# A hybrid decoder step on one core: score tiles spread over the ticks, low parts of q and k stored by their own stage, convolution rows joined, PV emptied by ScalarE alone

## What is computed

```python
q = rmsnorm(q, q_norm); k = rmsnorm(k, k_norm)            # per head, 16 heads of 64
logits = q @ k.T * ATTN_SCALE + bias                      # three dilated windows, merged
o = softmax(logits) @ v
out = sum(xpad[:, i:i + t] * conv_w[i] for i in range(4)) + conv_b
xbc = silu(out); z = silu(z)
```

## Time and profile before

| | us |
|---|---|
| median of 3 runs (2239.98 to 2244.58) | 2243.39 |
| the profiled execution | 2248.43 |
| span of its trace | 2245.8 |
| TensorE busy | 2100.7 (94%) |
| VectorE busy | 1047.1 (47%) |
| ScalarE busy | 588.3 (26%) |
| POOL busy | 840.3 (37%) |
| mean granted TensorE clock, share of 2.4 GHz | 0.971 |

### The profile page before, as it was taken

The page is one execution under the profiler, slowest core; times in us unless marked ns, Lnnn a source line. Parts: engine busy times, 40 slices in busy tenths (PEclk is TensorE's granted clock), DMA queues, the critical chain, the costliest instruction groups (busy, mean ns, idle before and its releaser), DMA issues. The chain is left out here.

```text
span 2245.8 us, 30116 instructions
## 1 busy us (share of the span) xinstructions
PE 2100.7 (94%) x12136; PEld 1845.0 (82%) x12136; DVE 1047.1 (47%) x1452; ACT 588.3 (26%) x1055; POOL 840.3 (37%) x494
## 2 busy tenths in 40 slices
PE   8999997898888899699998899999999999999999
PEld 7999996677777778345454678999999999999999
DVE  5888605778787665235443655252222122221222
ACT  4333223544455554232322201121101011010110
POOL 3564304646656655122211212333333333333332
PEclk9999998999999999789999899999999999999999
DMA  4333315333233341854744443311111111111112
GB/s 157 122 140 144 124 50 122 93 102 90 86 104 100 104 114 33 261 173 156 261 162 172 161 169 113 123 34 57 38 47 47 47 47 37 47 47 47 47 37 96
DMA packets 102756, 230.70 MB, mean 103 GB/s; under 512 B 17195, under 2 KB 50475, under 8 KB 101116
## 3 DMA queue, kind: packets, MB, share of 16 engines
q1 hardware_dynamic: 90252, 188.38, 26.8%
q10 hardware_dynamic: 12400, 40.90, 5.0%
HBM read 187.52 MB, written 50.29 MB: 106 GB/s over the span
## 5 line engine op out<-in xcount | busy, mean ns | idle before, releaser
L818 POOL TENSOR_SCALAR att_p<-att_p,att_rden 128x128 f32<-128x128 f32 (+7 forms) x128 | 229.3, 1793 | 227.1 <-DVE att_rden L916 226.9
L1847 POOL CAST wo_hi<-wo_raw 128x1024 fp32r<-128x1024 f32 x64 | 66.8, 1043 | 492.3 <-issue 239.4
L2171 ACT ACTIVATE r_sq<-stage 128x1056 f32<-128x1056 f32 x32 | 34.8, 1088 | 623.7 <-DVE stage L2360 623.7
L1849 POOL TENSOR_TENSOR wo_lo<-wo_raw,wo_hi 128x1024 fp32r<-128x1024 f32 x64 | 187.7, 2933 | 5.1
L1051 ACT ACTIVATE att_p<-att_p,att_min 128x128 f32<-128x128 f32 (+7 forms) x128 | 99.4, 776 | 152.0 <-DVE att_min L933 151.8
L921 DVE TENSOR_TENSOR att_pTlo<-att_t_ps,att_pThi 128x512 fp32r<-128x512 f32 x192 | 106.2, 553 | 54.9 <-ACT att_pThi L1059 52.8
L843 PE MATMUL dense_ps<-u_hi,w_hi 128*128 128x352 f32 x480 | 120.4, 353 | 11.7 <-DVE silu_half L961 4.7
L1059 ACT ACTIVATE att_pThi<-att_t_ps 128x512 fp32r<-128x512 f32 x192 | 92.0, 479 | 94.9 <-PE att_t_ps L872 94.0
L843 PE MATMUL dense_ps<-u_hi,w_lo 128*128 128x352 f32 x480 | 113.1, 345 | 0.0
L843 PE MATMUL dense_ps<-u_lo,w_hi 128*128 128x352 f32 x480 | 113.0, 346 | 0.0
L611 DVE RECIPROCAL proj_rinv<-proj_rinv 128x1056 f32<-128x1056 f32 x16 | 108.0, 6753 | 9.8 <-ACT proj_rinv L504 9.8
(11 more groups left out here) (307 smaller groups left out, 5355.6 us busy)
## 6 DMA issues: line engine op xcount, KB each, us to landing
sa_k<-in_cache_k SPq DMA_DIRECT2D x32, 640.0 KB, 9.2
sa_v<-in_cache_v SPq DMA_DIRECT2D x40, 512.0 KB, 7.0
w_raw<-in_w_feat SPq DMA_DIRECT2D x36, 512.0 KB, 6.1
wo_raw<-in_w_up SPq DMA_DIRECT2D x32, 512.0 KB, 3.5
wo_raw<-in_w_down SPq DMA_DIRECT2D x32, 512.0 KB, 3.5
out_qk<-proj_out ACTq DMA_DIRECT2D x16, 528.0 KB, 10.1
tmp_bias_rows<-tmp_table ACTq DMA_DIRECT2D x8, 1024.0 KB
att_q<-out_qk SPq DMA_DIRECT2D x32, 256.0 KB, 4.7
```

Of the source, the lines that this page charges most:

```text
L818: pool.tensor_scalar(slot(h, qt), slot(h, qt), rden[:, qt, :], None, ALU.mult).then_inc(normed, 1)
L1849: pool.tensor_tensor(w_lo[:, j], raw_w, w_hi[:, j].bitcast(F32), ALU.subtract).then_inc(f_split[j], 1)
```

## The change

- The score tiles move: qt 0 and 1 in tick 4, 2 and 3 in tick 5, qt 7 in tick 7, 4 in tick 9, 5 in tick 10, 6 in tick 12. qt 7 has two slots of its own (even and odd heads). A tile's number in the semaphores is now `rank`.
- `project` also makes a high copy of each normed q and k tile (ScalarE), subtracts it (POOL, `split_qk`) and stores the low part to a new DRAM tensor `qk_low` (ScalarE's queue). `split_k` and `split_q` are gone from VectorE. `weave` loads the raw tile in partitions 0 to 63 and the low tile in 64 to 127, for k and q. ScalarE makes four copies per head where it made two. The first product takes q's high part twice against k's high and low part, the second q's low part against k's high part over 64 rows (the product low x low is gone). The number of matmuls and their columns stay.
- The convolution's sample columns stand behind the prompt columns in one buffer of 1083 columns, so that a tap is one VectorE instruction over 1080 columns; the small copies of past and tail rows go to POOL (`pad`, `keep_tail`). The four taps of a tile go to the least loaded of the five ticks after its eviction.
- The product with zeros is gone: the last piece's product of the high part closes the accumulation. ScalarE copies both halves of PV (`split_out`), TensorE waits for those copies (`o_split`), and VectorE adds them later from SBUF.
- The order in a tick: VectorE `keep_low`, `bias_min`, `invert`, `evict`, `add_out`, `split_v`, taps, gates; ScalarE `split_out`, `keep_high`, `exponent`, casts, tanh, stores.
- The last z tile's tanh, gate and store run in three column groups.
- project and weave are two parts for the semaphores; POOL clears project's in tick 0 of `weave`.

```diff
@@ project
+                def split_qk(t):
+                    pool.wait_ge(highs_made, t + 1)
+                    if t >= 1:
+                        pool.wait_ge(lows_stored, 16 * t)
+                    pool.tensor_tensor(lows[:], outs[:, t % 2, 0:SEQ], high[:].bitcast(F32),
+                                       ALU.subtract).then_inc(lows_made, 1)
...
                 for n in range(3, NQ + 1):
                     ring.split_part(kit, pool, n, 0, 1)
+                    if n >= 4:
+                        split_qk(n - 4)
                     split_sq(n - 2)
...
                 def store(t):
                     act.wait_ge(normed, t + 1)
                     act.dma_start(dram["qk"][t * P:(t + 1) * P, :], outs[:, t % 2, :]).then_inc(qk_stored[t % 2], 16)
+                    if t >= 1:
+                        act.wait_ge(lows_made, t)
+                    act.activation(high[:], outs[:, t % 2, 0:SEQ], ACT.Copy).then_inc(highs_made, 1)
+
+                def store_low(t):
+                    act.wait_ge(lows_made, t + 1)
+                    act.dma_start(dram["qk_low"][t * P:(t + 1) * P, :], lows[:]).then_inc(lows_stored, 16)
...
                     evict(t)
+                    if t >= 3:
+                        store_low(t - 3)
                     store(t - 2)
...
                     if t >= 2:
                         dve.wait_ge(qk_stored[t % 2], 16 * (t // 2))
+                        dve.wait_ge(lows_made, t - 1)
@@ weave
+RANK = (0, 1, 2, 3, 5, 6, 7, 4)
+SCORE_TICK = (4, 4, 5, 5, 9, 10, 12, 7)
+SLOTS = (0, 128, 384, 768, 1280, 1920, 2688, 3584, 4608)
...
-            n = TICKS * (h - 1) + 5 + qt if qt < HALF else TICKS * (h - 1) + 5 + qt
-            score[n] = (h, qt)
+        for qt in sorted(range(NT), key=lambda q: RANK[q]):
+            score.setdefault(TICKS * (h - 1) + SCORE_TICK[qt], []).append((h, qt))
...
+    for d in range(ND):
+        evict_at.setdefault(made_at[d], []).append(d)
+        last = made_at[d]
+        if d < NX:
+            free = sorted(range(last + 1, last + 6), key=lambda n: (busy[n], n))[0:WIDTH]
...
-                    for rows in (slice(0, HD), slice(HD, P)):
-                        sp.dma_start(q_raw[rows, :], dram["qk"][f * P + r:f * P + r + HD, 0:SEQ]).then_inc(qk_loaded, 16)
...
+                        sp.wait_ge(qk_cast, 4 * h)
+                    for buf, first in ((k_raw, D + f * P + r), (q_raw, f * P + r)):
+                        sp.dma_start(buf[0:HD, :], dram["qk"][first:first + HD, 0:SEQ]).then_inc(qk_loaded, 16)
+                        sp.dma_start(buf[HD:P, :], dram["qk_low"][first:first + HD, :]).then_inc(qk_loaded, 16)
...
+                    for d in evict_at.get(n - 1, ()):
+                        if d < NX:
+                            keep_tail(d)
+                    for d in tanh_at.get(n, ()):
+                        if d + 1 < NX:
+                            pad(d + 1)
...
+                    if n == 0:
+                        kit.clear(pool)
...
-                def scores(s, h, qt):
+                def scores(h, qt):
+                    free = NT * h + max(qt - 1, 0) if qt < HALF else rank(h, qt)
                     if qt == 0:
-                        pe.wait_ge(qk_split, h + 1)
+                        pe.wait_ge(qk_cast, 4 * (h + 1))
+                    if free:
+                        pe.wait_ge(biased, free)
...
-                        pe.matmul(s_ps[:, base + c:base + c + cw], q, k_hi[:, c:c + cw], start=True, stop=False)
-                        mm = pe.matmul(s_ps[:, base + c:base + c + cw], q, k_lo[:, c:c + cw], start=False, stop=True)
+                        pe.matmul(out, q_high[:, qt * P:w], k_two[:, c:c + cw], start=True, stop=False)
+                        mm = pe.matmul(out, q_low[:, qt * P:w], k_two[0:HD, c:c + cw], start=False, stop=True)
...
-                            pe.wait_ge(o_kept, 2 * h + g)
+                            pe.wait_ge(o_split, 2 * h + g)
...
-                    if b == HALF * (g + 1) - 1:
-                        mm = pe.matmul(pv_ps[:], nought[:], x_hi[:, 0, 0:512], start=False, stop=True)
+                    if last:
+                        mm = pe.matmul(pv_ps[:, off:512], v_two[:, h % 2, b, :], p_hi[:, m % 3, off:512],
+                                       start=False, stop=True)
...
-                    dve.tensor_tensor(oT[h % 2 * HD:(h % 2 + 1) * HD, g * 512:(g + 1) * 512], pv_ps[0:HD, :], o_part[:],
-                                      ALU.add).then_inc(o_kept, 1)
+                    dve.tensor_tensor(oT[h % 2 * HD:(h % 2 + 1) * HD, g * 512:(g + 1) * 512], o_parts[:, 0, :],
+                                      o_parts[:, 1, :], ALU.add).then_inc(o_kept, 1)
...
-                        dve.scalar_tensor_tensor(out=acc_p, in0=pre[:, t:t + SEQ], scalar=w, in1=acc_p,
-                                                 op0=ALU.mult, op1=ALU.add)
-                        dve.scalar_tensor_tensor(out=acc_s, in0=pre_s[:, :, t:t + T_DEC], scalar=w, in1=acc_s,
-                                                 op0=ALU.mult, op1=ALU.add).then_inc(conv, 1)
+                        dve.scalar_tensor_tensor(out=half[:, 0:CONV], in0=pre[:, t:t + CONV], scalar=w,
+                                                 in1=half[:, 0:CONV], op0=ALU.mult, op1=ALU.add).then_inc(conv, 1)
...
-                def split_k(h):
-                    dve.wait_ge(qk_cast, 2 * h + 1)
-                    dve.tensor_tensor(k_lo[:], k_raw[:], k_hi[:].bitcast(F32), ALU.subtract)
-
-                def split_q(h):
-                    dve.wait_ge(qk_cast, 2 * h + 2)
-                    dve.tensor_tensor(q_two[HD:P, :], q_raw[HD:P, :], q_two[HD:P, :].bitcast(F32),
-                                      ALU.subtract).then_inc(qk_split, 1)
...
-                    act.activation(o_part[:], pv_ps[HD:P, :], ACT.Copy).then_inc(o_split, 1)
+                    act.activation(o_parts[:, 0, :], pv_ps[0:HD, :], ACT.Copy)
+                    act.activation(o_parts[:, 1, :], pv_ps[HD:P, :], ACT.Copy).then_inc(o_split, 1)
...
-                    act.activation(k_hi[:], k_raw[:], ACT.Copy).then_inc(qk_cast, 1)
-
-                def cast_q(h):
-                    act.activation(q_two[:], q_raw[:], ACT.Copy).then_inc(qk_cast, 1)
+                    act.activation(k_two[:], k_raw[:], ACT.Copy).then_inc(qk_cast, 1)
+
+                def cast_q(h, rows):
+                    act.activation(q_high[rows, :], q_raw[0:HD, :], ACT.Copy).then_inc(qk_cast, 1)
+
+                def cast_q_low(h):
+                    act.activation(q_low[:], q_raw[HD:P, :], ACT.Copy).then_inc(qk_cast, 1)
...
+                        act.dma_start(rows[:, 0:SEQ], half[:, 0:SEQ]).then_inc(feat_stored, 16)
+                        act.dma_start(rows[:, SEQ:NTOK].rearrange("p (b t) -> p b t", b=NB_DEC),
+                                      sample(half)[:, :, 0:T_DEC]).then_inc(feat_stored, 16)
```

More of the change, by code:

```diff
@@ L265, in project @@
         out = outs[:, 0, :]
+        high, lows = sb("qk_high", [P, SEQ], F32R), sb("qk_low", [P, SEQ])
         x_eps = sb("x_eps", [P, NTOK])
@@ L676, in weave, with rank, width @@
     UNITS = 3 * KD
-    order = {s: 8 * h + qt for s, (h, qt) in score.items()}
+    END = LAST + 12
+    def rank(h, qt):
+        return NT * h + RANK[qt]
+    def width(n):
+        _, g, b = piece[n]
+        return P * (HALF - max(b - HALF * g, 0))
     def pe_cost(n):
@@ L713, in weave, with stores @@
                 made_at[d] = n
-    at = {}
-    for d, n in made_at.items():
-        at.setdefault(n, []).append(d)
-    starts = {}
-    for d in range(1, ND):
-        starts[made_at[d - 1]] = d
-    END = LAST + 9
+    starts = {made_at[d - 1]: d for d in range(1, ND)}
+    ends = {n + 3: piece[n][0:2] for n in piece if piece[n][2] == HALF * (piece[n][1] + 1) - 1}
+    busy = dict.fromkeys(range(FIRST, END + 1), 0.0)
+    for n in busy:
+        if n in piece:
+            busy[n] += 0.16 + 0.00104 * width(n)
+        busy[n] += sum(0.18 + 0.134 * (qt + 1) for _, qt in score.get(n, ()))
+        busy[n] += 0.16 * len(score.get(n - 1, ())) + 0.69 * (n in ends) + 0.7 * (n % TICKS == 9)
+    for d in range(ND):
+        busy[made_at[d]] += 1.7
+    evict_at, tap_at, tanh_at, gate_at, store_at = ({} for _ in range(5))
+    for d in range(ND):
+        evict_at.setdefault(made_at[d], []).append(d)
+        last = made_at[d]
+        if d < NX:
+            free = sorted(range(last + 1, last + 6), key=lambda n: (busy[n], n))[0:WIDTH]
+            for t, n in enumerate(sorted(free)):
+                tap_at.setdefault(n, []).append((d, t))
+                busy[n] += 1.3
+                last = n
+        tanh_at.setdefault(last + 1, []).append(d)
+        gate_at.setdefault(last + 2, []).append(d)
+        busy[last + 2] += 1.27
+        store_at.setdefault(last + 3, []).append(d)
+    def stores(d):
+        return 16 * (min(d, NX) + d) + 32 * max(d - ND + 1, 0)
     with ExitStack() as mem:
@@ L762, in slot, with sample @@
         def slot(h, qt):
```

(35 more changed lines are left out.)

227 lines of the change are left out of this document (108 added, 119 removed).

## The result

The changed kernel is **slower**: 2301.73 us (median of 4 runs, 2298.45 to 2305.90) against 2243.98 (4 runs, 2239.98 to 2252.41) of the kernel before beside it, a ratio of 1.0253 with a 95% interval of 1.0217 to 1.0289. The forecast was 2173, with a range up to 2210. The profiled execution has a span of 2304.1 us at a mean granted clock of 0.967, against 2245.8 at 0.971.

A forecast was written before the change was run, and what follows sets the result against it. VectorE, 80% busy and otherwise standing behind ScalarE, was taken to bound weave's ticks. Savings of 21, 14.6, 9.0, 5, 12, 9.6 and 1 us, less 2 added, made -70: from 2243.4 to 2173 us, range 2140 to 2210.

The forecast's parts named there:

- Part 8: Project: the added ScalarE copy, transfer issue and POOL subtraction per q or k tile cost 0, between 0 and 17 us.
- the mean of L615: Sign in project: if this scaling product's mean rises by over 1 us, the pricing of project's added work is wrong.
- the rival in which the subtraction holds VectorE back: Project: POOL's new subtraction lengthens VectorE's loop by 1.1 us a tile, 17 us in all; 2190 us, chance 0.12.
- Part 4: Weave: dropping 32 products with zeros saves TensorE 9.0 us; the second score product's 64 rows count at nothing.
- Part 2: Weave: spread score tiles and new tick order cut TensorE's bias-step waits by 21 us and most of VectorE's exponential waits.
- the first rival: Weave: VectorE goes on pacing the heads, its waits for ScalarE only moving; 40 us gained, 2203 us, chance 0.22.
- Part 3: Weave: ScalarE empties PV, so TensorE no longer waits for VectorE; 0.8 us left in each of 15 heads, -14.6 us.
- a PV wait above 20 us: Sign in weave: TensorE's wait for the PV bank this long would show the step on ScalarE emptying PV wrong.
- The rival in which ScalarE becomes the bound: Weave: ScalarE gets 52.5 us more work and sets each head; kernel slower by 43.5, 2287 us, chance 0.04.
- Parts 5, 6 and 7: Weave: eviction waits -5 us, cost of waits beyond their record -12, half the lost clock regained -9.6.
- Part 6: Weave: each wait costs TensorE some 0.25 us beyond its record; 48 of 70 waits go, -12 us.
- Part 1: Weave: splits, sample taps and wider taps take 60 us off VectorE, its worth showing only in the waits.

The follow-up runs named there:

- a_both: Changed kernel with the second score product over 128 rows (zero-padded) and low transfers issued by SyncE: 2225.78 us, ratio 0.9893 against the kernel before.
- d_cast: c_pv with one of the two casts of a head's first tick moved to the second: 2197.86 us, ratio 0.9767 against the kernel before.
- c_pv: a_both with the old emptying of PV (one ScalarE copy, VectorE adding out of PSUM at the head of its tick): 2211.09 us.
- d_skew: c_pv with the 1 MB bias transfers issued from SyncE's queue instead of ScalarE's: 2239.75 us.
- a_sp: Changed kernel with the low transfers issued by SyncE instead of ScalarE, same single buffer: 2264.52 us, ratio 1.0064 against the kernel before.
- a_two: Changed kernel with two low buffers in turn, transfers still in ScalarE's queue: 2262.37 us, ratio 1.0052 against the kernel before.

## Why the prediction was wrong, by its own steps

**Part 8 failed, and it is the largest error.** It priced the copy, the subtraction and an issue in project at 0, with 17 at worst, and asked only whether POOL and VectorE had room and where ScalarE's copy stands. It left out the wait that the change adds: POOL's subtraction waits for the landing of the previous low part, with the splits of squares and weights behind it, and that transfer stands in ScalarE's queue behind 1 MB of bias rows. That cost 52.7 us, 41 of which came back with another queue. The test it named for itself, the mean of L615, pointed the other way: 2.67 us before, 2.49 for its successor. So the rival in which the subtraction holds VectorE back is not what happened either.

**Part 4 failed in its last sentence.** "That the second one uses 64 rows I count at nothing" was a price of 0, with no bounds, for a change of form that the weave of before does not show. 192 pairs cost 44 to 46 us in the new arrangement and 15 in the old, where more was hidden. The Trainium skill, "TensorEngine Tiling (Array Packing)", section "Key Properties", says that a change of tiling mode drains TensorE. The rows at 600 us fit that, in both directions; that the 0.2 us are such a drain is not shown. A search for a rule against the change would have found it and given it a chance. The zeros themselves, forecast at -9.0, were worth nothing that could be measured in either arrangement: -5.1 and +2.4 on putting them back (-3.6 and +3.6 by ratio).

**Part 2 was right in direction, too small.** Old ticks cost 14.2, the old order 28.1; if they add, which no run tried, 42, against -21. VectorE's wait for exponentials fell to 26.0 and 27.7, not below 15, and VectorE's waits for ScalarE as a whole did not fall: 133 us before, 135 in a_both, of which 107.1 for high copies. That is what the first rival had named, waits that only move to other instructions. TensorE's wait for the bias step, which I took as the test, misled: 14.1 in the changed kernel came with a slow TensorE, and 29.5 in a_both with a fast one. The time of a stretch is the test, not one wait in it.

**Part 3 had the wrong sign**: +14.7 instead of -14.6. It counted the wait that goes and left 0.8 us a head for ScalarE, and did not count who waits for ScalarE's tick. The test it named, a PV wait above 20 us, did not catch it (14.4 in the changed kernel, 18.7 in a_both). The rival in which ScalarE becomes the bound named this work, and asked for an engine that is never idle; it is enough that an engine on which others wait is late in its tick.

**Parts 5, 6 and 7.** Evictions: 6.1 us wait in the changed kernel, 10.7 in a_both, against 3. The clock of the first stretch came to 0.99, a little better than the 0.97 forecast. Part 6 was not measured by itself, and Part 1, the work taken off VectorE, has no run of its own.

**The sum.** With both causes removed (a_both) the kernel is 24 us under the one before, by ratio, where 70 were forecast: the form of the product and the queue account for 81 of the 128 us between the forecast and the measured time. Undoing the PV part gives 15 more and moving one cast 11, so that d_cast's weave is 61.5 us shorter than before, 511.8, near the forecast of 503, but by another way: without the PV part, and with a cast moved that the forecast did not name. What is left beside the forecast is mostly the 12 us in project. The bias transfers in ScalarE's queue stood in the profile of before, and products over 64 rows were nowhere in its weave; both I had set to 0 instead of bounding them. The rival at 2287 us lies near the 2302 measured by luck: in it ScalarE sets each head, and ScalarE was 59% busy from 440 to 693 us.

## What to carry to other kernels

When a step moves a store, write down the chain behind it: which buffer waits for its landing, which engine waits on that buffer, what is queued behind that wait, and what large transfer shares its queue. A product over fewer rows than its neighbours can cost more than one over all rows, as here, and filling the rest with zeros can be faster; price any form that the trace does not show from both sides. And judge a change by the length of its stretch, since a wait shrinks as well when the waiting engine gets slower.

## What the runs showed of the hardware that was not expected

In weave's `float32r` products each change between 128 and 64 rows costs about 0.2 us, whatever the width: 512 columns take 0.43 us from start to start against 0.22 with 128 rows throughout, 256 columns 0.31 against 0.12. The 128\*64 form of the low PV product, with all rows and half of the output columns, shows no such cost: in c_pv its mean is 340 ns, beside 375 of its 128\*128 neighbours, and in the kernel before such a product of 512 columns at 414.43 us was followed by the next at 414.66. Nor is it seen in the plain fp32 products of the mixers: before, four over 128 rows start at 1154.03, four over 32 rows at 1155.89, and the next at 1157.74, so 1.86 and 1.85 us for four products of 512 columns each.

An issue that usually takes 0.33 us was held behind a 1 MB transfer with reversed rows in the same queue, and what stood behind it in that engine's order waited. In the changed kernel three issues of a low part came 5.6 us after that of a bias transfer and took 8.01, 10.08 and 5.39 us; the other five that followed one came 10 us and more after it and took 0.32 to 1.54. The distance is not the whole of it: in c_pv the issue of a store 12 us behind one took 7.14. On SyncE (d_skew) an issue right behind one took 11.68. With the two kinds in separate queues (a_sp) the low parts landed in 6.3 to 8.3 us; in one queue in 2.6 to 24.7 in the changed kernel, and in up to 28.0 in a_two.
